# A projection made in halves of 256 columns instead of halves of the contraction, in a gated hybrid layer on one NeuronCore

## What is computed

```python
xn = _rmsnorm(x, g_pre)
u = xn @ w_in                       # (tokens, 1024) @ (1024, IN_WIDTH): the projection
gq, gk, gv, gg, glr, dq, dk, dv, dg, ga, gb = jnp.split(u, cuts, axis=-1)
o_a, s_new = _gla(q, k, v, log_a, gla_s0)            # gated linear attention
y_a = (rmsnorm(o_a) * silu(gg)) @ w_gla_branch
o_b = softmax_over_groups(lse) * dilated windows     # three groups, four heads
y_b = (o_b * silu(dg)) @ w_dil_branch
merged = sigmoid(ga) * y_a + sigmoid(gb) * y_b
h = x + _rmsnorm(merged @ w_out, g_post)
h = h + (pe @ w_ple_proj) * sigmoid(h @ w_ple_gate)
```

## Time and profile before

| | us |
|---|---|
| median of 3 runs (2802.44 to 2805.39) | 2802.55 |
| the profiled execution's own time | 2802.39 |
| its span, first to last instruction | 2800.5 |
| TensorE busy in it | 2769.0 |

### The profile page before, as it was taken

The page is one execution under the profiler, slowest core; times in us unless marked ns, Lnnn a source line. Parts: engine busy times, 40 slices in busy tenths (PEclk is TensorE's granted clock), DMA queues, the critical chain, the costliest instruction groups (busy, mean ns, idle before and its releaser), DMA issues.

```text
span 2800.5 us, 40579 instructions
## 1 busy us (share of the span) xinstructions
PE 2769.0 (99%) x16108; PEld 1453.2 (52%) x16108; DVE 1077.7 (38%) x2401; ACT 860.8 (31%) x1728; POOL 383.9 (14%) x633
## 2 busy tenths in 40 slices
PE   8999999999999999999999999999999899999998
PEld 4444456555545665666555555555544344444444
DVE  6211134444333443344223333333322655555452
ACT  5111124444312222343123321111112534444441
POOL 2000011111311002120011114333200100000000
PEclk9999999999999999999999999999999999999999
DMA  9543464655577566584576779777646966556642
GB/s 281 135 165 133 148 208 152 214 175 202 197 251 287 187 194 214 184 274 152 178 278 209 256 234 290 250 247 254 217 152 220 282 171 173 148 149 181 164 112 58
DMA packets 319886, 558.35 MB, mean 199 GB/s; under 512 B 179114, under 2 KB 184305, under 8 KB 315218
## 3 DMA queue, kind: packets, MB, share of 16 engines
q1 hardware_dynamic: 268722, 290.57, 34.8%
q0 software_dynamic: 50544, 258.89, 27.8%
q10 hardware_dynamic: 432, 6.29, 0.5%
HBM read 378.70 MB, written 236.79 MB: 220 GB/s over the span
## 4 chain that ended last, share of the span: by engine, by line
PE 96%; DMA 2%; SPq 1%; DVE 1%; ACT 0%; issue 0%; POOL 0%; DVEq 0%; POOLq 0%
PE out L2646 40%; PE out L2212 22%; PE out L2643 18%; PE out L1143 2%; PE out L1128 2%; PE out L2649 2%; PE out L1134 1%; PE out L615 1%; PE out L625 1%; PE out L626 1%; PE out L1432 1%; PE out L1392 1%; DMA mix_pe_in<-in_p_prompt 1%; SPq L356 1%; PE out L1117 1%; PE out L1405 0%
## 5 line engine op out<-in xcount | busy, mean ns | idle before, releaser
L2646 PE MATMUL out<-w_hi,xn_hi 128*128 128x512 f16 x1792 | 680.0, 379 | 1.1 <-DVE w_lo L2511 0.6
L2646 PE MATMUL out<-w_lo,xn_hi 128*128 128x512 f16 x1792 | 679.6, 379 | 0.0
L2646 PE MATMUL out<-w_hi,xn_lo 128*128 128x512 f16 x1792 | 679.5, 379 | 0.0
L2542 ACT ACTIVATE stage<-out 128x512 f32<-128x512 f32 (+1 forms) x170 | 99.3, 584 | 929.2 <-PE out L2646 615.5
L2584 DVE TENSOR_SCALAR stage<-out 128x512 f32<-128x512 f32 (+1 forms) x170 | 114.7, 675 | 644.9 <-PE out L2646 398.3
L2643 PE MATMUL out<-xn_hi,w_hi 128*128 128x512 f16 x768 | 291.4, 379 | 0.0
L2643 PE MATMUL out<-xn_hi,w_lo 128*128 128x512 f16 x768 | 291.1, 379 | 0.0
L2643 PE MATMUL out<-xn_lo,w_hi 128*128 128x512 f16 x768 | 291.1, 379 | 0.0
L2646 PEld LDWEIGHTS out<-w_hi,xn_lo 128*128 128x128 f16 x1792 | 175.3, 98 | 211.6 <-issue 0.3
L2646 PEld LDWEIGHTS out<-w_hi,xn_hi 128*128 128x128 f16 x1792 | 175.7, 98 | 192.8 <-issue 6.2
L2646 PEld LDWEIGHTS out<-w_lo,xn_hi 128*128 128x128 f16 x1792 | 175.4, 98 | 186.4 <-issue 0.3
(11 more groups left out here) (321 smaller groups left out, 3974.1 us busy)
## 6 DMA issues: line engine op xcount, KB each, us to landing
out<-in_cache_kv_w POOLq DMA_DIRECT2D x64, 1020.0 KB, 9.8
U<-stage SPq DMA_DIRECT2D x224, 256.0 KB, 4.7
raw<-in_w_in SPq DMA_DIRECT2D x78, 512.0 KB, 5.1
UT<-stage SPq DMA_DIRECT2D x96, 256.0 KB, 4.2
sw_kc<-in_cache_kv_w POOLq DMA_DIRECT2D x24, 1024.0 KB, 12.2
sw_vc<-in_cache_kv_w POOLq DMA_DIRECT2D x24, 1024.0 KB, 9.1
sw_rows<-U POOLq DMA_DIRECT2D x32, 512.0 KB, 7.1
out<-in_cache_kv_w POOLq DMA_DIRECT2D x16, 1008.0 KB, 8.3
```

The source lines that it names most:

```text
L2542: move_out(act, m, lambda o, x: act.activation(o, x, ACT.Copy, scale=1.0 / W_SCALE))
L2646: last = pe.matmul(out[m % 3][:, :], x[:, k, at:at + P], y[:, k, :], start=first, stop=final)
```

## The change

Three edits. (1) A prompt tile's first slot now makes columns 0 to 255 of the tile over the whole contraction, and the second slot columns 256 to 511. So each matmul moves 256 columns instead of 512, and each stationary block is loaded once in either slot. The sample tile stays as it was. (2) The waits follow: at a column tile's start all four weight pieces are waited for ahead of the first slot, and in the first column tile both units of a token tile. (3) `turn_z` of token tile 2 is taken out of `queue(sp, 1)`, where it stood behind the wait for the stores and behind `load_x`, and put ahead of that wait.

```diff
         if self.has(t + 1):
-            self.turn_z(sp, t + 1)
+            if t > 1:
+                self.turn_z(sp, t + 1)
...
                 mix.queue_before(sp, q, stores)
+            mix.turn_z(sp, 2)
             stores.wait_tiles(sp, COLUMN_TILES)
...
                 if n < COLUMN_TILES:
-                    if t == 0:
-                        pe.wait_ge(lo_ready, n * PIECES + (half + 1) * PIECES // SLOTS)
-                    if n == 0:
-                        inputs.wait_half(pe, t, half)
+                    if t == 0 and half == 0:
+                        pe.wait_ge(lo_ready, (n + 1) * PIECES)
+                    if n == 0 and half == 0:
+                        for i in range(SLOTS):
+                            inputs.wait_half(pe, t, i)
...
-                    for k in range(half * K_TILES // SLOTS, (half + 1) * K_TILES // SLOTS):
+                    part = slice(half * HALF, (half + 1) * HALF)
+                    for k in range(K_TILES) if rows == P else range(half * K_TILES // SLOTS, (half + 1) * K_TILES // SLOTS):
...
-                                last = pe.matmul(out[m % 3][:, :], y[:, k, block * P:(block + 1) * P], x[:, k, group * BANK:(group + 1) * BANK],
-                                                 start=first, stop=final)
+                                tokens = slice(group * BANK + half * HALF, group * BANK + (half + 1) * HALF)
+                                last = pe.matmul(out[m % 3][:, part], y[:, k, block * P:(block + 1) * P], x[:, k, tokens], start=first, stop=final)
                             elif rows == P:
-                                last = pe.matmul(out[m % 3][:, :], x[:, k, at:at + P], y[:, k, :], start=first, stop=final)
+                                last = pe.matmul(out[m % 3][:, part], x[:, k, at:at + P], y[:, k, part], start=first, stop=final)
```

## The result

The changed kernel takes 2827.21 us (median of 4 runs, 2825.04 to 2827.55) against 2802.83 us (4 runs): ratio 1.0084, 95% interval 1.0072 to 1.0096. It is 24.4 us slower; 2825 was forecast.

What follows compares the result with a forecast made beforehand. TensorE, busy for 2769.0 of 2800.5 us, was taken as the bound. 19.2 + 2.9 + 0.9 - 0.3 - 0.4 = 22.3 us on the profiled 2802.39 gave 2824.7, stated as 2825 us, range 2818 to 2836.

Steps and rivals of the forecast that it cites:

- The split, 19.2 us: In the projection's prompt part, 7680 more matmuls, each with a weight load, cost 2.5 ns each: 19.2 us slower.
- The weight load is no bound: In the projection, a 256-column matmul covers its 98 ns weight load; the rival that it doesn't, 2876, had chance 0.08.
- The fourth piece, 2.9 us: In the first column tile TensorE starts only when the fourth weight piece is done, at about 17.9 instead of 15.07: +2.9 us.
- The clock at the start, 0.9 us: Behind the longer first pause the projection's half clock costs 1.5 us instead of 0.6: +0.9 us, between 0 and 2.
- The absorbed wait, -0.3: The 0.5 us wait for a turned token tile in the first column tile may partly go: -0.3 us, between -0.5 and 0.
- The moved transposes, -0.4: Token tile 2's z transposes go out no earlier, but ahead of two loads of x: -0.4 us, between -0.8 and +1.1.
- What held z: Token tile 2's transposes waited for z, which began when its loads landed, 19.22 us after issue, not for the stores.

Runs made afterwards that it cites:

- the two halves under one block: Kernel before, with 22 of a tile's 24 matmuls made as two of 256 columns behind each other with the same stationary block: 2819.35 us against 2803.63.
- the split with waits by piece: Changed kernel, but in a column tile's first slot TensorE waits for each weight piece, and the second token unit, only ahead of the steps reading it: 2821.40 us against 2803.16.
- The table of eight kernels: Eight kernels leaving the order of loads and weights alone, with or without the third edit: last z load 18.89 to 21.30 us to landing, TensorE's wait 8.6 to 11.2.

## Why the prediction was right, point by point

- **The split, 19.2 us: right.** The stretch behind the first tile grew by 19.4 us. Step distance 0.1091 us against the 0.1092 taken; the two halves under one block give 15.7 to 17.3 us for 17.6 expected; the split with waits by piece, which also starts earlier, 18.2.
- **The weight load is no bound: right**, and by far for the float16 loads of the projection: they are hidden at 0.0558 us as well. The Trainium skill (TensorE: Matmul & The Clock Gate) has two statements that this bears on. Its section on the 2.5 ns above the columns gives 55.6 ns for 128 columns and 215.7 for 512, for matmuls back to back; here 55.8 and 215.8 hold with a load to each, so the trace agrees. Its section on the back-to-back gap gives 81 and 131 ns for a stream with loads; the trace agrees with neither.
- **The fourth piece, 2.9 us: right.** The wait grew from 0.59 to 3.30 us in the kernel that has only the new waits, 2.7 us. In the changed kernel's profile the start came 2.1 us later, since its weights happened to land 0.8 us earlier (7.71 against 8.49).
- **The clock at the start, 0.9 us: about right on average, 0.6 too small in this pair of profiles.** The changed kernel's starts are 0.21 us apart from 17.15 to 21.39, 4.25 us at 1.2 GHz, 2.1 us lost; less the 0.6 of before, 1.5 us. Over all profiles the difference is 1.1 us. What the prediction didn't see is that the 0.6 of before is no fixed amount: kernels with the same start lose 0 to 2.4 us.
- **The absorbed wait, -0.3: not borne out.** The wait for the turned token tile is 0.8 us where it was 0.5. The chain that feeds these tiles starts with the eviction of TensorE's first tile, as the prediction said itself, and moved along with it. But the 0.3 us are no measure of the change: the split without the third edit waits 0.3 us there, and kernels with the start of before 0.2 to 0.7.
- **The moved transposes, -0.4: right that it is next to nothing**; the kernel with this edit alone is at 0.9999. That it also shortens the transposes' way was not seen here: 4.29 us to landing against 4.12. In the changed kernel the wait for z was 1.3 us longer for another reason: the loads landed after 20.26 us, not 19.22, as they did in kernels without this edit. The half clock behind it lasted longer too (granted clock 0.50 for 4.76 us instead of 3.05), which makes up the last 0.9 us.
- **What held z: right.** It is the landing of its own loads beside the weights. The table of eight kernels shows the wait following that landing. Where these loads came early, the data was ready before the stores had landed, and the third edit began to count.

Sum against measurement: 22.3 forecast; 24.4 by the medians, 25.0 by the two spans. The 2.7 us between are 0.6 from the clock at the start, 0.6 from the absorbed wait, and some 2.3 from the later landing and the slow clock at z, less 0.8 from the luck of the first landing. Of these parts none is tied to the change by a run; they lie within what alike kernels show at the same places. The mechanism of the forecast held, and that the sum came within 2.1 us is in part luck, since its parts outside of the split can differ by as much from one execution to the next.

## What to carry to other kernels

Price a split of matmuls by the distance of starts in a stream, not by busy time: on this kernel each extra matmul cost 2.5 ns, which is nothing once and 19 us when 7680 come in on the engine that is never idle. Before moving a transfer ahead of a wait, look at whose end its issue coincides with: here it was the data, not the wait, and the same edit was worth 0 us or 6.3 us depending on that. Before giving a microsecond at one place of one profile to an edit, look at the same place in a kernel that doesn't have the edit. And a transfer moved out of a crowd puts another one in: look which transpose now meets the weights before counting the gain.

## What the runs showed of the hardware that I had not expected

- At 128 columns a matmul the start distance stayed at 0.0558 us with a 98 ns weight load to each in the profile, so by its rows loads overlap each other as well as the matmuls. The float32 load of 0.19 us behind such a matmul was not hidden: it added 0.05 us, 53 times.
- At that density TensorE stopped four times, 8.0 us in all, with no releaser in the profile. At 256 columns its list of waits has no such stop.
- In the kernel that has only the new waits the clock did not fall in the pause of 3.3 us but 0.9 us after work had resumed (18.59), and stayed low until about 21.9. A pause can so be paid behind its end. With the same start, other executions lost between 1.6 and 2.8 us to it.
- The granted clock in the profile is not always that of the work: it is 1.00 over 4.25 us of the changed kernel in which matmuls start at the distance of 1.2 GHz.
